# Other staging space for the second half of the latent tiles, and other release points for turned keys, queries and values

## The chip, the cores and the metric

One Trainium2 chip; the program runs on 8 cores, each with its own share of the work and none waiting for another. The time of a run is that of the slowest core, in device microseconds. A profile of one execution is at hand, and three timed runs.

## The reference

One layer of a hybrid diffusion transformer, cut to what matters:

```python
sh1, sc1, g1, sh2, sc2, g2 = adaln(c, w_ada, b_ada)      # silu(c) @ w_ada + b_ada, in six parts
h = rms_norm(x, norm1_w) * (1 + sc1) + sh1
q, k, v, u, g = split(h @ w_in)                          # 1024, 1024, 1024, 1024, 1024 columns
q, k = rope(rms_norm64(q)), rope(rms_norm64(k))          # the context's: no rope; its k and v are outputs
# 8 heads, each with two softmax maps of 64 dimensions; latents read their own and 256 cached keys
att = sublayer_rms((softmax(q1 @ k1.T / 8) - lam * softmax(q2 @ k2.T / 8)) @ v)
sgu = gelu(u) * (w_s @ layer_norm(gelu(g)) + b_s)        # in chunks of 128 positions
x = x + g1 * (concat(att, sgu) @ w_o)
h = rms_norm(x, norm2_w) * (1 + sc2) + sh2
x = x + g2 * (square(relu(h @ w_ff1)) @ w_ff2)
```

There are 16 context sequences of 256 tokens and 4 latent sequences of 2048, model width 2048. Two cores share a latent sequence: each computes the outputs of its own 1024 latent tokens and of two context sequences.

## The kernel before, in words

**Tiles.** A core has 12 own tiles of 128 tokens: 0 to 3 context, 4 to 11 its own latents. For attention it also needs keys and values of the *other half* of its latent sequence, tiles 12 to 19. These are loaded (`x_load`), normed (`norm_x`: a square on ScalarE with its sum, a reciprocal root, a scale on ScalarE, VectorE or GpSimd), transposed on TensorE and modulated (`late_group`, groups of two: 12, 14, 16, 18) into `hO`, and projected to keys and values only. `group_ev[t]` tells that group t stands in `hO`, `xnev[t]` that tile t is normed.

**Stages.** First modulation (`ada0`: 8 units of 4 pieces of weights, from a ring of 6 buffers of 4 KB per partition at address b0) beside the first projection (`proj0`), which runs over four quarters of the contraction and keeps partial sums of pair 0's keys and queries (`KU`), and of pair 0's and 1's values (`VU`), in SBUF; `drained[...]` tells that such a sum has been read for the last time. Then the four groups of the other half with pair 0's k and v, and pair 1's values by `late_v1` wherever TensorE has time (priority 15; `proj0` has 14, the smaller number goes first). Then for the pairs of heads 0 to 3 `attention(p)` beside `proj(p+1)`; then the gates, the output projection and the MLP. The weights for `proj(1)` go where those of `proj0` were: each block of 1 MB is loaded when group 18's matmuls with the old one are through.

**Turns.** A projected and normed key or query tile lies in one of 8 buffers (`kr`) and is transposed by a DMA of SyncE, a *turn* (`S.turn`), into `KT[s]` or `QT[s]`; s is the pair's number modulo 2. `VV[s]` holds values. Before a turn (or a write of values) for pair p >= 2 the chain waits for `att_end[p-2]`, that is all of attention p-2 with its last `finalize`. `sc_end[p]` is the end of its scores, `av_done[p]` that of its products with values.

**Space.** Slot 0 at b0 holds KT0 (11 KB), QT0 (6 KB), VV0 (11 KB); slot 1 behind it, KT1, QT1, VV1, then z1 and p1. `xt` are the loads' buffers (8 KB each), `xn` those of normed tiles (4 KB). For tiles 12 to 19 the buffers come one after the other from the pools in `xpool`: `xta` (xt0, under `hO[3]`), `xtb` (xt1, under `hO[2]`, once four partial sums of values are drained), `xtp` (xt4 and xt5 at p1, under the probabilities, once keys' and queries' sums are drained). The loads leave from one thread in the order of the tiles; GpSimd issues them.

**Order.** Nothing is ordered by hand: `Sched` simulates threads with costs in ns while the program is built. A thread posts instructions to engines; each engine takes the one of least priority number that is ready in the simulation, and that order is fixed in the program. On the chip each engine runs its list in order, and semaphores are derived from the memory that instructions read and write. A turn is costed at 300 + 1.7 ns per element of a row, a transfer at 315 B/ns, and a turned tile of pair 0 counts as there 8 us after its turn (`TURN_SLACK`).

Lines that matter: L586 issues loads, L591 stores, L597 turns; L455 is every matmul, L465 every transpose of TensorE; L488 ScalarE, L510 and L517 VectorE, L543 GpSimd's scale.

Of the kernel before, what the change touches and what calls it, by code (L numbers as in the profile page):

```python
# [9 lines left out]
F32 = mybir.dt.float32  # L10
BF16 = mybir.dt.bfloat16
# [4 lines left out]
D = 2048  # L16
# [4 lines left out]
K = 1024  # L21
SB = 16512
# [600 lines left out]
def build_program():  # L623
# [34 lines left out]
    S = Sched(nc)  # L658
# [4 lines left out]
    def bank(j):  # L663
        return PS[:, j * 512:(j + 1) * 512]
# [44 lines left out]
    b0 = SB + 118 * K  # L709
    KT, QT, VV = [], [], []  # L710
    for i in range(2):
        b = b0 + i * SLOT
# [3 lines left out]
    slot1 = b0 + SLOT  # L716
    z1 = b0 + 2 * SLOT
# [16 lines left out]
    NPART = 6  # L734
    ada = [S.sbuf("ada%d" % i, [128, 4, 512], BF16, b0 + i * 4 * K) for i in range(NPART)]
    adas = Pool(S, range(NPART))
    xt = [S.sbuf("xt%d" % i, [128, D], F32, b) for i, b in enumerate((SB + 86 * K, SB + 78 * K, slot1 + 17408, z1 + 4 * K, p1, p1 + 8 * K))]
    xts = Pool(S, range(4))
    xta, xtb, xtp = Pool(S), Pool(S), Pool(S)
    xpool = [xts] * 12 + [xta, xtb, xta, xtb, xtb, xta, xta, xtp]  # L740
    xn = [S.sbuf("xn%d" % i, [128, D], BF16, slot1 + i * 4 * K) for i in (2, 3, 0, 1)]
    xns, xno = Pool(S, range(4)), Pool(S)
    mod0 = S.sbuf("mod0", [128, 512], F32, z1)
    cT_t = S.sbuf("cT_t", [128, 16, 2], F32, z1 + 2048)
# [17 lines left out]
    def evs(n):  # L762
        return [Ev() for _ in range(n)]
# [11 lines left out]
    ada_ev, xev, xnev, raw_ev = [evs(4) for _ in range(8)], evs(20), evs(20), evs(12)  # L775
    mod_ev, h_ev = evs(4), [evs(3) for _ in range(4)]
    sc_ev, ident_ev, const_ev, tab_ev, lam_ev = Ev(), Ev(), Ev(), Ev(), Ev()
    own_x, ho_free, slot1_ev, wr2_ev, ada_out = Ev(), evs(4), Ev(), Ev(), Ev()
    group_ev = {t: Ev() for t in range(12, 20, 2)}
    W0 = {(k, b): Ev() for k in ("k0", "v0", "q0", "v1") for b in range(4)}  # L780
# [63 lines left out]

    def staging():
        xta.give(0)
        yield [drained[k] for k in VU[:4]]
        xtb.give(1)
        yield [drained[k] for k in KU[:4]]
        xtp.give(4)  # L850
        yield [drained[k] for k in KU[4:8]]
        xtp.give(5)
        yield [drained[k] for k in KU[8:]]
        xno.give(2)
        xno.give(3)
        yield xnev[12:20] + [group_ev[18]]
        slot1_ev.fire()
# [41 lines left out]
    def ada0():  # L899
        yield [sc_ev, const_ev]  # L900
        for u in range(8):
            j = yield banks
            for i in range(4):
                yield ada_ev[u][i]
                op = ada_mm(ada[adabuf[u, i]], bank(j), 512, range(4 * i, 4 * i + 4), 4 * i)
                op.then(lambda u=u, i=i: adas.give(adabuf[u, i]))
            yield op
            yield S.copy(mod0, bank(j))
            yield from ada_cols(mod0, bank(j), 512, 1 if u % 2 == 0 else 0, (u // 2) * 4, 0)
            banks.give(j)  # L910
            if u % 2 == 1:
                mod_ev[u // 2].fire()
# [73 lines left out]
    def chain_qk(b, kind, t0, p, op):  # L986
# [71 lines left out]
                yield S.spawn(rope(zn, kind, t0 - 4, rb if early else None), 23 if p else RP + (1 if kind == 'q' else 0))  # L1058
            stats.give(st)
        dst = QT[s] if kind == "q" else KT[s]  # L1060
        yield att_end[p - 2 if p >= 2 else 4]
        if p == 1:
            yield slot1_ev
        yield S.turn(dst[:, t0:t0 + 2].rearrange("p t h n -> p (t h) n"), zn, "kr%d" % kj)
        krs.give(kj)
        if p == 0:
# [42 lines left out]

    def chain_v(b, t0, p, op):  # L1110
        s = p % 2
        yield [op, att_end[p - 2 if p >= 2 else 4]]
        dst = VV[s][:, t0:t0 + 2, :, 0:128]
        v4 = lambda a: a.rearrange("p (t h d) -> p t h d", t=2, h=2)
        sv_rows = sv[t0 * 128:(t0 + 2) * 128, p * 256:(p + 1) * 256].rearrange("(t p) n -> p t n", p=128) if t0 < 4 else None
        if t0 < 4:
            vf = yield outs[p]
            yield S.copy(vf, bank(b))
            banks.give(b)
            yield S.copy(dst, v4(vf))  # L1120
        else:
            yield S.copy(dst, v4(bank(b)))
            banks.give(b)
        VVev[p][t0 // 2].fire()
        if t0 < 4:
            S.store(sv_rows, vf.rearrange("p (t n) -> p t n", t=2), "sk").then(lambda: S.at(STORE_SLACK if p else 0.0, lambda: outs[p].give(vf)))

    def cached(p):
        s = p % 2
        yield att_end[p - 2 if p >= 2 else 4]  # L1130
        if p == 1:
            yield own_x
        ops = [S.memset(VV[s][:, :, :, 128:130], 1.0)]
        for t in range(2):
            ops.append(S.load(VV[s][:, 20 + t, :, 0:128], cv[t * 128:(t + 1) * 128, p * 256:(p + 1) * 256].rearrange("p (h d) -> p h d", d=128),
                              "cv%d" % t, cast=True))
        kj = yield krs
        ops.append(S.load(kr[kj].rearrange("p (t n) -> p t n", t=2), ck[:, p * 256:(p + 1) * 256].rearrange("(t p) n -> p t n", p=128),
                          "ck", cast=True))
        yield ops  # L1140
        VVev[p][10].fire()
        yield S.turn(KT[s][:, 20:22].rearrange("p t h n -> p (t h) n"), kr[kj], "kr%d" % kj)
        krs.give(kj)
        KTev[p][10].fire()
# [79 lines left out]
        op.then(v_done.fire)  # L1224

    def half_free(h):
        yield [drained[k] for k in VU[4 * h + 4:4 * h + 8]] if h < 2 else xnev[12:17] if h == 2 else xnev[12:19]
        ho_free[h].fire()

    ORD = "kqv"  # L1230
# [107 lines left out]
    def attention(p):  # L1338
        s = p % 2
        yield [sc_end[p - 1], QTev[p][0], tab_ev]  # L1340
        if p == 0:
            yield [proj_end[0]] + xnev
            for i in range(3):
                Ps.give(i)
            yield (banks, range(6))
# [10 lines left out]
        def av():  # L1356
            yield av_done[p - 1]
            n = 0
            while n < len(items):
                if not todo:  # L1360
                    more[0] = Ev()
                    yield more[0]
                    continue
                its, pj, es = todo.popleft()
                yield [VVev[p][it[2] // 2] for it in its] + es
                ops = []
                for j, (hh, q0, kt, first, last) in enumerate(its):
                    if first:
                        if ops:
                            S.mm(ops)  # L1370
                            ops = []
                        yield Otok
                    for m in range(2):
                        for i in range(2):
                            ops.append((O[m][:, i * 130:i * 130 + 129], Pt[pj][:, m, j * 256 + i * 128:j * 256 + (i + 1) * 128],
                                        VV[s][:, kt, hh, 0:129], first and i == 0, last))
                    if last:
                        op = S.mm(ops)
                        ops = []
                        fin.append(S.spawn(finalize(2 * p + hh, q0, op), 8))  # L1380
                if ops:
                    op = S.mm(ops)
                op.then(lambda pj=pj: Ps.give(pj))
                n += len(its)

        av_end = S.spawn(av(), 10.5)
        for i0 in range(0, len(items), 4):
# [67 lines left out]
    def gates():  # L1455
# [11 lines left out]
        for n, (nb, t0) in enumerate(GORD):  # L1467
            yield wev[4, nb]
            w = wslot[4, nb]
            if t0 < 4:  # L1470
                yield att_end[2]
            j = yield banks
            for i in range(2):
                for k0 in range(0, 16, 4):
# [438 lines left out]
```

How the kernel before makes its waits and increments, by code:

```python
    def add(self, eng, fn, reads=(), writes=(), key=None, dr=(), dw=()):  # L204
# [63 lines left out]
            for s, v in nd.snap.items():  # L268
                if known.get(s, 0) < v:
                    known[s] = v
            known[nd.sem] = nd.val
        E = self.eng[eng]
        wl = list(waits.items())
        attach = None
        if eng != "pe" and wl:
            attach = wl.pop()
        for s, v in wl:
            E.wait_ge(self.sems[s], v)
        ins = fn(E)
        if attach:
            ins._wait_ge(self.sems[attach[0]], attach[1])
        nd = Node()
        nd.eng = eng
        nd.dma = dma
        if dma:
            name = "d_" + key
            if name not in self.sems:
                self.sems[name] = self.nc.alloc_semaphore(name)
                self.dcnt[name] = 0
            self.dcnt[name] += 1
            ins.then_inc(self.sems[name], 16)
            nd.sem, nd.val = name, 16 * self.dcnt[name]
        else:
            self.cnt[eng] += 1
            ins.then_inc(self.esem[eng], 1)
            nd.sem, nd.val = "c_" + eng, self.cnt[eng]
        nd.snap = dict(known)
        i = len(self.nodes)
# [301 lines left out]
    def wait_all_stores(self, keys):  # L600
        for k in keys:
            nd = self.nodes[self.dlast[k]]
            if self.known["sp"].get(nd.sem, 0) < nd.val:
                self.nc.sync.wait_ge(self.sems[nd.sem], nd.val)
```

## Time and profile before

| what | value |
|---|---|
| three timed runs | 2464.01, 2472.96, 2458.88 us; median 2464.01 |
| the profiled execution | 2466.38 us |
| its span on the slowest core, core 4 | 2465.3 us |
| spans of all cores | 2444.4 to 2465.3 us |
| TensorE matmul busy | 2366.6 us (96%) |
| VectorE, ScalarE, GpSimd busy | 1120.7 (45%), 729.1 (30%), 232.5 us (9%) |
| DMA | 251.58 MB, mean 102 GB/s |

Shares are means over the whole span: TensorE is far less busy in the first 300 us than after. L12 is line 12 of the kernel. "PE" is TensorE's matmul, "PEld" its weight load, "DVE" VectorE, "ACT" ScalarE, "POOL" GpSimd, "SP" SyncE, "SPq" a DMA issue on SyncE. Releasers of waits are inferred from semaphores.

### The profile page before, as it was taken

The numbers are of one execution on the slowest core, as the hardware profiler recorded it, in microseconds if no ns is written. First come the engines' busy times: TensorE is split into PE (matmuls) and PEld (weight loads), VectorE is DVE, ScalarE is ACT, GpSimd is POOL, SyncE is SP. The second block draws the span as 40 slices with busy tenths as digits, with TensorE's granted clock in tenths as the row PEclk, the third lists the DMA queues.
The fourth block names the chain that finished last, engine by engine and source line by source line (L and its number), as shares of the span: only waits on it lengthen the run. The fifth ranks groups of instructions, "written<-read, shape, count | busy, mean of one in ns | idle before, by whom it ended". The sixth has DMA issues, their size and how long they took to land.

```text
span 2465.3 us, 38569 instructions; the slowest of 8 cores (2444.4 to 2465.3 us)
## 1 busy us (share of the span) xinstructions
PE 2366.6 (96%) x16224; PEld 1357.6 (55%) x16224; DVE 1120.7 (45%) x2216; ACT 729.1 (30%) x1196; POOL 232.5 (9%) x394
## 2 busy tenths in 40 slices
PE   3689799999999999999999999999999999999999
PEld 2568687878888854444444444444444444444444
DVE  2567776744742154554101332322524616528347
ACT  2515576766756561222231001001010010010110
POOL 1213311111111030000110000000000000000000
PEclk9799899999999999999999999999999999999999
DMA  9995978967754285976563333333433434434346
GB/s 217 191 170 139 120 97 90 128 95 111 117 85 85 45 125 134 241 210 129 93 108 52 52 52 52 52 52 52 90 65 60 89 55 71 80 51 84 63 96 187
DMA packets 168729, 251.58 MB, mean 102 GB/s; under 512 B 101104, under 2 KB 106864, under 8 KB 154480
## 3 DMA queue, kind: packets, MB, share of 16 engines
q0 software_dynamic: 54816, 169.14, 42.3%
q1 hardware_dynamic: 113744, 79.97, 14.0%
q8 instruction: 132, 2.16, 0.4%
q14 instruction: 37, 0.30, 0.0%
HBM read 348.28 MB, written 32.67 MB: 155 GB/s over the span
## 4 chain that ended last, share of the span: by engine, by line
PE 91%; DMA 5%; DVE 2%; ACT 1%; issue 0%; POOL 0%; SPq 0%
PE ps L455 91%; DMA ada<-wa 2%; DMA QT<-kr 1%; DMA sk<-t 1%; DMA xt<-xp 1%; PE ps L465 1%; DMA wr<-wa 1%; DVE hT L517 0%; DVE xn L517 0%; DMA tab<-rsin 0%; ACT xn L488 0%; DMA sv<-t 0%; DVE t L510 0%; ACT hO L488 0%; POOL xn L543 0%
## 5 line engine op out<-in xcount | busy, mean ns | idle before, releaser
L455 PE MATMUL ps<-wf,aT 128*128 128x512 bf16 x3072 | 665.0, 379 | 0.0
L455 PE MATMUL ps<-hT,wf 128*128 128x512 bf16 x3072 | 665.0, 379 | 0.0
L455 PEld LDWEIGHTS ps<-wf,aT 128*128 128x128 bf16 x3072 | 300.3, 98 | 362.3 <-issue 0.8
L455 PEld LDWEIGHTS ps<-hT,wf 128*128 128x128 bf16 x3072 | 300.2, 98 | 362.4 <-issue 0.8
L488 ACT ACTIVATE tm<-ps 128x512 f32<-128x512 f32 x192 | 114.4, 597 | 1030.0 <-PE ps L455 1030.0
L510 DVE TENSOR_TENSOR aT<-tm 128x512 bf16<-128x512 f32 x192 | 132.7, 692 | 549.3 <-ACT tm L488 546.5
L455 PE MATMUL ps<-wr,hT 128*128 128x256 bf16 x2880 | 356.7, 280 | 19.6 <-DVE hT L517 15.8
L488 ACT ACTIVATE P<-ps 128x1024 bf16<-128x1024 f32 x304 | 296.5, 1020 | 148.6 <-PE ps L455 148.5
L455 PEld LDWEIGHTS ps<-wr,hT 128*128 128x128 bf16 x2880 | 280.8, 100 | 70.5 <-issue 33.9
L510 DVE TENSOR_TENSOR acc<-acc,ps 128x512 f32<-128x512 f32 x216 | 148.4, 687 | 154.2 <-PE ps L455 153.8
L455 PE MATMUL ps<-VV,P 128*128 128x129 bf16 x2432 | 166.0, 221 | 6.2 <-issue 3.3
L510 DVE TENSOR_TENSOR tm<-ps,g_t 128x512 f32<-128x512 f32 x168 | 115.9, 690 | 95.1 <-PE ps L455 94.9
L455 PEld LDWEIGHTS ps<-VV,P 128*128 128x128 bf16 x2432 | 141.8, 98 | 30.3 <-issue 29.7
L586 POOL DMA_DIRECT2D wf<-wf x64 | 33.9, 530 | 1185.1 <-PE ps L455 1150.7
L455 PE MATMUL ps<-wr,hO 128*128 128x256 bf16 x1024 | 121.3, 273 | 1.3 <-ACT hO L488 0.8
L455 PEld LDWEIGHTS ps<-wr,hO 128*128 128x128 bf16 x1024 | 97.2, 98 | 16.3 <-issue 5.8
L455 PE MATMUL ps<-QT,KT 64*128 64x256 bf16 x1216 | 93.2, 272 | 2.2 <-ACT P L488 1.8
L455 PE MATMUL ps<-hT,wu 128*128 128x512 bf16 x384 | 85.8, 379 | 0.0
L455 PE MATMUL ps<-wo,sguT 128*128 128x512 bf16 x384 | 84.8, 379 | 0.0
L510 DVE TENSOR_TENSOR acc<-acc,tm 128x512 f32<-128x512 f32 x120 | 82.9, 691 | 3.6
L586 POOL DMA_DIRECT2D wr<-wa x96 | 51.3, 551 | 297.2 <-PE ps L455 296.9
L465 PE MATMUL ps<-identb,xn 128*128 128x128 bf16 x320 | 30.3, 270 | 43.3 <-DVE xn L517 29.8
(177 smaller groups left out, 1610.9 us busy)
## 6 DMA issues: line engine op xcount, KB each, us to landing
wf<-wf POOLq DMA_DIRECT2D x64, 1024.0 KB, 9.9
wr<-wa POOLq DMA_DIRECT2D x96, 256.0 KB, 7.5
ada<-wa POOLq DMA_DIRECT2D x32, 512.0 KB, 22.0
xt<-xs POOLq DMA_DIRECT2D x16, 1024.0 KB, 8.8
x1d<-xw SPq DMA_DIRECT2D x12, 1024.0 KB, 5.7
x1b<-x1d SPq DMA_DIRECT2D x48, 256.0 KB, 3.0
wr<-wqkv POOLq DMA_DIRECT2D x44, 256.0 KB, 11.2
wo<-wo POOLq DMA_DIRECT2D x32, 256.0 KB, 9.9
```

What stands on the lines that cost most here:

```text
L455: ins = e.matmul(o, lhsT=l, rhs=r, start=st, stop=sp, skip_group_check=True)
L465: ins = e.transpose(o, i, ident)
L488: "act", lambda e: e.activation(out=out, in_=in_, func=func, bias=bias, scale=scale, **kw),
L510: return self.post(eng, cost, lambda: self.add(eng, lambda e: e.tensor_tensor(out=out, in0=a, in1=b, op=op), reads=[a, b], writes=[out]), ...
L586: eng, lambda e: e.dma_start(out=out, in_=src), writes=[out], key=key, dr=dr), 0, nbytes=nb, prio=prio)
```

## The change

* The fifth load buffer `xt4` moves from p1 to b0, where the first two ring buffers of the modulation are (later KT0); `xt5` goes. A pool `xtc` hands it out when the last modulation matmul is through (`ada_done`). Tiles 12 to 19 come from xta, xtc, xtb, xtc, xta, xtb, xtc, xta.
* Two more buffers for normed tiles, xn4 and xn5, at b0 + 8 KB and b0 + 12 KB (later the end of KT0, and QT0), also from `ada_done` on.
* So the turns of pair 0 wait: early keys for `xnev[18]`; queries, late keys and the cached key for `group_ev[18]`. `hO[2]` and `hO[3]` become free one normed tile later. `attention(0)` waits for all of `KU` to be drained.
* For pairs 2 and 3 turns wait for `sc_end[p-2]`, writes of values for `av_done[p-2]`, the gates' first tiles for `av_done[2]`; `av_done` now follows the end of the last product.

```diff
--- before.py
+++ after.py
@@ -734,11 +734,12 @@
     NPART = 6
     ada = [S.sbuf("ada%d" % i, [128, 4, 512], BF16, b0 + i * 4 * K) for i in range(NPART)]
     adas = Pool(S, range(NPART))
-    xt = [S.sbuf("xt%d" % i, [128, D], F32, b) for i, b in enumerate((SB + 86 * K, SB + 78 * K, slot1 + 17408, z1 + 4 * K, p1, p1 + 8 * K))]
+    xt = [S.sbuf("xt%d" % i, [128, D], F32, b) for i, b in enumerate((SB + 86 * K, SB + 78 * K, slot1 + 17408, z1 + 4 * K, b0))]
     xts = Pool(S, range(4))
-    xta, xtb, xtp = Pool(S), Pool(S), Pool(S)
-    xpool = [xts] * 12 + [xta, xtb, xta, xtb, xtb, xta, xta, xtp]
+    xta, xtb, xtc = Pool(S), Pool(S), Pool(S)
+    xpool = [xts] * 12 + [xta, xtc, xtb, xtc, xta, xtb, xtc, xta]
     xn = [S.sbuf("xn%d" % i, [128, D], BF16, slot1 + i * 4 * K) for i in (2, 3, 0, 1)]
+    xn += [S.sbuf("xn%d" % i, [128, D], BF16, b0 + (4 * i - 8) * K) for i in (4, 5)]
     xns, xno = Pool(S, range(4)), Pool(S)
     mod0 = S.sbuf("mod0", [128, 512], F32, z1)
     cT_t = S.sbuf("cT_t", [128, 16, 2], F32, z1 + 2048)
@@ -775,6 +776,7 @@
     ada_ev, xev, xnev, raw_ev = [evs(4) for _ in range(8)], evs(20), evs(20), evs(12)
     mod_ev, h_ev = evs(4), [evs(3) for _ in range(4)]
     sc_ev, ident_ev, const_ev, tab_ev, lam_ev = Ev(), Ev(), Ev(), Ev(), Ev()
+    ada_done = Ev()
     own_x, ho_free, slot1_ev, wr2_ev, ada_out = Ev(), evs(4), Ev(), Ev(), Ev()
     group_ev = {t: Ev() for t in range(12, 20, 2)}
     W0 = {(k, b): Ev() for k in ("k0", "v0", "q0", "v1") for b in range(4)}
@@ -844,12 +846,12 @@
 
     def staging():
         xta.give(0)
+        yield ada_done
+        xtc.give(4)
+        xno.give(4)
+        xno.give(5)
         yield [drained[k] for k in VU[:4]]
         xtb.give(1)
-        yield [drained[k] for k in KU[:4]]
-        xtp.give(4)
-        yield [drained[k] for k in KU[4:8]]
-        xtp.give(5)
         yield [drained[k] for k in KU[8:]]
         xno.give(2)
         xno.give(3)
@@ -905,6 +907,8 @@
                 op = ada_mm(ada[adabuf[u, i]], bank(j), 512, range(4 * i, 4 * i + 4), 4 * i)
                 op.then(lambda u=u, i=i: adas.give(adabuf[u, i]))
             yield op
+            if u == 7:
+                ada_done.fire()
             yield S.copy(mod0, bank(j))
             yield from ada_cols(mod0, bank(j), 512, 1 if u % 2 == 0 else 0, (u // 2) * 4, 0)
             banks.give(j)
@@ -1058,9 +1062,11 @@
                 yield S.spawn(rope(zn, kind, t0 - 4, rb if early else None), 23 if p else RP + (1 if kind == 'q' else 0))
             stats.give(st)
         dst = QT[s] if kind == "q" else KT[s]
-        yield att_end[p - 2 if p >= 2 else 4]
+        yield sc_end[p - 2 if p >= 2 else 4]
         if p == 1:
             yield slot1_ev
+        if p == 0:
+            yield group_ev[18] if kind == "q" or t0 >= 12 else xnev[18]
         yield S.turn(dst[:, t0:t0 + 2].rearrange("p t h n -> p (t h) n"), zn, "kr%d" % kj)
         krs.give(kj)
         if p == 0:
@@ -1109,7 +1115,7 @@
 
     def chain_v(b, t0, p, op):
         s = p % 2
-        yield [op, att_end[p - 2 if p >= 2 else 4]]
+        yield [op, av_done[p - 2 if p >= 2 else 4]]
         dst = VV[s][:, t0:t0 + 2, :, 0:128]
         v4 = lambda a: a.rearrange("p (t h d) -> p t h d", t=2, h=2)
         sv_rows = sv[t0 * 128:(t0 + 2) * 128, p * 256:(p + 1) * 256].rearrange("(t p) n -> p t n", p=128) if t0 < 4 else None
@@ -1127,7 +1133,7 @@
 
     def cached(p):
         s = p % 2
-        yield att_end[p - 2 if p >= 2 else 4]
+        yield av_done[p - 2 if p >= 2 else 4]
         if p == 1:
             yield own_x
         ops = [S.memset(VV[s][:, :, :, 128:130], 1.0)]
@@ -1139,6 +1145,8 @@
                           "ck", cast=True))
         yield ops
         VVev[p][10].fire()
+        if p == 0:
+            yield group_ev[18]
         yield S.turn(KT[s][:, 20:22].rearrange("p t h n -> p (t h) n"), kr[kj], "kr%d" % kj)
         krs.give(kj)
         KTev[p][10].fire()
@@ -1224,7 +1232,7 @@
         op.then(v_done.fire)
 
     def half_free(h):
-        yield [drained[k] for k in VU[4 * h + 4:4 * h + 8]] if h < 2 else xnev[12:17] if h == 2 else xnev[12:19]
+        yield [drained[k] for k in VU[4 * h + 4:4 * h + 8]] if h < 2 else xnev[12:18] if h == 2 else xnev[12:20]
         ho_free[h].fire()
 
     ORD = "kqv"
@@ -1339,7 +1347,7 @@
         s = p % 2
         yield [sc_end[p - 1], QTev[p][0], tab_ev]
         if p == 0:
-            yield [proj_end[0]] + xnev
+            yield [proj_end[0]] + xnev + [drained[k] for k in KU]
             for i in range(3):
                 Ps.give(i)
             yield (banks, range(6))
@@ -1382,6 +1390,7 @@
                     op = S.mm(ops)
                 op.then(lambda pj=pj: Ps.give(pj))
                 n += len(its)
+            yield op
 
         av_end = S.spawn(av(), 10.5)
         for i0 in range(0, len(items), 4):
@@ -1468,7 +1477,7 @@
             yield wev[4, nb]
             w = wslot[4, nb]
             if t0 < 4:
-                yield att_end[2]
+                yield av_done[2]
             j = yield banks
             for i in range(2):
                 for k0 in range(0, 16, 4):
```

## Rows read from the trace of the kernel before

**Rows 1.** Spans and granted clock of the cores, the slowest.
```profile
core 4: 2465.3 us, clock 0.986
```

**Rows 2.** Stretch, length, busy PE, PEld, DVE, ACT, POOL; clock, DMA share, GB/s.
```profile
200.00:230.00 30.00, 26.79 (x252) 23.92 (x250) 21.89 (x46) 19.30 (x40) 14.00 (x11) 0.89 0.49 151
230.00:260.00 30.00, 22.32 (x217) 19.53 (x216) 21.51 (x34) 21.03 (x47) 10.22 (x8) 0.91 0.61 115
260.00:300.00 40.00, 31.38 (x270) 24.81 (x269) 31.47 (x72) 20.66 (x46) 18.16 (x22) 0.88 1.07 112
...
400.00:600.00 200.00, 195.30 (x2444) 157.44 (x2444) 110.17 (x342) 134.53 (x204) 36.20 (x66) 0.99 0.75 104
600.00:800.00 200.00, 199.99 (x2408) 164.16 (x2405) 102.60 (x311) 128.72 (x199) 26.29 (x48) 1.00 0.61 98
```

**Rows 3.** TensorE's waits, 200 to 274 us: total, times, longest.
```profile
PE ps L465 <- ACT st L498: 6.2, 1, 6.2
PE ps L465 <- POOL xn L543: 3.2, 1, 3.2
PE ps L465 <- DVE xn L517: 1.1, 1, 1.1
```

**Rows 4.** TensorE in time: start, us, instructions, [idle before, releaser].
```profile
207.63 2.72 PE L465 MATMUL ps<-identb,xn 128*128 128x128 bf16 x24 [3.21 <-POOL xn L543]
...
224.90 11.95 PE L455 MATMUL ps<-wr,hO 128*128 128x256 bf16 x108
237.98 1.95 PE L465 MATMUL ps<-identb,xn 128*128 128x128 bf16 x32 [1.13 <-DVE xn L517]
...
258.13 3.41 PE L465 MATMUL ps<-identb,xn 128*128 128x128 bf16 x32 [6.24 <-ACT st L498]
...
279.36 7.76 PE L455 MATMUL ps<-wr,hT 128*128 128x256 bf16 x44 [2.35 <-DMA wr<-wqkv]
287.51 0.61 PE L455 MATMUL ps<-QT,KT 64*128 64x256 bf16 x8 [0.38 <-DMA QT<-kr]
```

**Rows 5.** TensorE's waits, 274 to 306 us.
```profile
PE ps L455 <- DMA wr<-wqkv: 3.4, 2, 2.4
PE ps L455 <- DVE ot L549: 2.7, 1, 2.7
```

**Rows 6.** GpSimd in time: its loads of x and one norm.
```profile
164.92 0.58 POOL L586 DMA_DIRECT2D xt<-xs  x1
191.47 0.53 POOL L586 DMA_DIRECT2D xt<-xs  x1 [25.97 <-DVE VV L510]
...
202.05 5.44 POOL L543 TENSOR_SCALAR xn<-xt,st 128x2048 bf16<-128x2048 f32 x1 [5.78 <-ACT st L498]
...
221.74 1.13 POOL L586 DMA_DIRECT2D xt<-xs  x2 [3.45 <-DVE xn L517]
```

**Rows 7.** Loads of x: landings of 60 to 320, then of 236 to 256 us.
```profile
DMA to landing us min/median/max: 5.2/7.5/22.8
...
L586 POOL DMA_DIRECT2D xt<-xs x2: 528/566/603, 238.1 to 239.3; - x2
...
DMA to landing us min/median/max: 9.8/11.7/13.5
```

**Rows 8.** VectorE in time: the last value sum of group 12's space.
```profile
204.13 0.69 DVE L510 TENSOR_TENSOR t<-ac_0v,ps 128x512 f32<-128x512 f32 x1 [1.74 <-DMA sv<-t]
```

**Rows 9.** Core 6, TensorE's waits, 180 to 420 us.
```profile
PE ps L455 <- DMA wr<-wqkv: 7.2, 2, 5.1
```

**Rows 10.** Turns: one issued at 266.7 us, then those of 269 to 286 us.
```profile
DMA to landing us min/median/max: 2.3/2.3/2.3
...
L597 SPq DMA_TRANSPOSE QT<-kr x4: 1190/1326/1502, 269.6 to 284.2; - x4
...
  DVE kr L510: 5.2, 1
...
DMA to landing us min/median/max: 13.2/15.5/17.8
```

## The prediction

> **What bounds the kernel now.** I read the spans and clocks of the cores first: core 4 is the slowest at 2465.3 us [rows 1]. The profiled execution took 2466.4 us, so 1.1 us lie outside the span; the median of the runs shown, 2464.0, is 2.4 us lower. The sum below is made for core 4 against 2466.4, and the 2.4 us are taken off at the end.
>
> Next came the busy time by stretches [rows 2]. From 600 us on TensorE is busy in 200.0 of 200 us, so whatever is saved ahead of that arrives whole at the end, and the later stretches read the same; nothing can be saved there by freeing a buffer. Between 200 and 300 us it is busy 26.8 + 22.3 + 31.4 = 80.5 of 100 us: 19.5 us stand open, at a granted clock of 0.88 to 0.91, that is for the most part at the upper of its two levels (2.4 GHz) and for some microseconds at the lower (1.2 GHz). This is where the tiles of the other half of the latents (x12 to x19) are normed, transposed and multiplied.
>
> Then the waits of TensorE in that stretch. Ahead of the transposes of groups 12, 14 and 18 it waits 3.2 + 1.1 + 6.2 = 10.5 us for normed tiles [rows 3]. The timeline puts them at 207.6, 238.0 and 258.1 us [rows 4]. After the last group it waits 3.4 us for the first weights of pair 1, 2.7 us for the attention's output accumulator [rows 5], and 0.4 us for a turned query ahead of the first score at 287.5 [rows 4].
>
> Why are the normed tiles late? GpSimd's timeline of loads [rows 6]: x12 is issued at 164.9 us. x13 waits 26.0 us, until 191.5, because its space (xt1) lies under four partial sums of values. x16 and x17 leave at 221.7, x18 and x19 at 238.1 and 239.3 [rows 7], each when a buffer has been normed (x19 when partial sums of keys have been drained). A load lands 5.2 us after its issue at best, 7.5 in the median [rows 7]. So two staging buffers, used by turns, set the pace; the DMA is not full (busy share 0.49 and 0.61 by the page's measure in those stretches [rows 2]).
>
> **The change, part by part.**
>
> 1. *A third staging buffer and two more places for normed tiles, in the ring of the first modulation.* xt4 moves to b0 and is free at ada_done, the end of the last modulation matmul. The last piece for that matmul is issued ahead of x12, on the same queue, and x12 lands at 164.9 + 22.8 = 187.7 [rows 6, 7]; so ada_done falls between 165 and 188, and I take 180. Then x13 leaves near 180 instead of 191.5, x14 near 191.5 as x13 did. With three buffers in turn and some 5.5 us for each load, x19 lands at about 187.7 + 7 x 5.5 = 226 us, against 239.3 + 13.5 = 252.8 [rows 6, 7]. The norms take about 4 us more each: x19 is ready at 230 or a little later, while TensorE, at 2 us of transposes and three projections of some 3.5 us (32 x 0.11, from 108 matmuls in 11.95 us [rows 4]) per group, comes to group 18 at 205 + 3 x 12.5 = 242 us. The wait of 6.2 and that of 1.1 us go: 7.4 us. Group 12 was held by a norm that GpSimd took for 5.44 us, until 207.5 [rows 6]; next late is the space of its output, which waits for the partial sum of a value that VectorE drains at 204.13 + 0.69 = 204.8 [rows 8]. I count 207.6 - 204.9 = 2.7 us. Bounds for these three waits: 3 us saved (the late norms of ScalarE and VectorE remain) to 10.5.
>
> 2. *The clock behind these waits.* After the two long ones the transposes run slower: at 207.6 us 24 took 2.72 us, 32 took 3.41 us at 258.1, where 32 took 1.95 us after a wait of 1.1 [rows 4]. That is 1.3 + 1.5 = 2.8 us, saved if the waits fall under some 1 us; bounds 0 and 5 (the projections right behind are slow as well).
>
> 3. *Weights of pair 1.* Their space comes free at group 18's last key projection, and only v18 and one late projection of pair 1's values cover the load. If tiles arrive ahead of TensorE, those late projections (priority 15, after 14) are left for the end and cover it. At stake: 3.4 us [rows 5] and the slow matmuls behind, 44 in 7.76 us instead of 44 x 0.11 = 4.9 [rows 4], 2.9 us; 6.3 in all. The other end: core 6 waits 7.2 us here today, 3.8 more than core 4 [rows 9]. I take 4 us saved, nearer to the gain, since the order by priority speaks for the cover.
>
> 4. *Turns wait longer.* Turned keys of pair 0 wait for xnev[18]; queries, the four late keys and the cached key for group_ev[18]. By part 1 xnev[18] comes at about 222 to 228, some 20 us ahead of the last group, so the six early keys are out of the way by then. Of the six queries four are turned from 269.6 on today [rows 10]. Now six queries, k12, k14, k16, k18 and the cached key, eleven turns, leave in one run after the last group. What is queued behind: SyncE's other stores (none urgent), and the chains that hold the 8 kr buffers; VectorE already stood 5.2 us for one [rows 10]. A turn alone lands in 2.3 us; the four issued between 269.6 and 284.2, beside three blocks of weights, took 13.2 to 17.8 [rows 10]. Cost between 0 (TensorE has pair 1's projections as filler, and everything is 12 us earlier) and 15 (see the second rival). I take 3, near the waits of 0.4 + 2.7 us of today.
> The Trainium skill says in "DMA: Bandwidth & Descriptors", Queues, rings and completion order, that an SDMA engine takes turns between queue rows packet by packet, so a turn with small packets gets a small part beside large loads. The trace agrees (2.3 against 13.2 to 17.8 us). By that rule the turns that start before the weights are quick and those behind them slow; with the 3 us counted for them the sum below is 13.9 us, and with turns that are never slowed 16.9.
>
> 5. *Attention of pair 0 also waits for all early keys and queries to be drained; its first probabilities no longer share space with x18 and x19.* Today the first score waits 0.4 us for a turned query [rows 4], so the drains behind these turns are earlier still. With kr buffers held longer the drains of the last queries follow the first key turns, at about 240 to 250, ahead of the end of projection 0 (about 260). Nothing; if it were late, projections of pair 1 cover it. Bounds 0 and 3.
>
> 6. *sc_end and av_done for att_end (pairs 2 and 3, first gate tiles), and the step that waits for the last value product.* These open buffers one finalize earlier, at 500 us and later, where TensorE has no open time [rows 2]. Between 400 and 600 it is open for 4.7 us [rows 2], and a buffer of attention could have been behind 2 of them at most. Nothing; bounds 2 saved, 1 lost, since instructions change their order.
>
> Sum: 7.4 + 2.7 + 2.8 + 4 - 3 = 13.9 us. 2466.4 - 13.9 = 2452.5, less 2.4: **2450 us**, 0.57% faster. The whole of the 19.5 open us and the slow clock would be some 25.
>
> **The rivals.**
>
> *The pace is not set by space.* Norms wait in the queues of ScalarE and VectorE (the 6.2 us are put down to ScalarE's statistics [rows 3]), and GpSimd may again be given a norm of 5.4 us. For it: VectorE is busy 21.9 and 21.5 of 30 us there [rows 2]. Against it: those statistics came 2 us after a tile that landed at 252.8. Then about half of parts 1 and 2 comes, 5 to 6 us, and part 3 stays away: 2459.
>
> *The waits move behind the last group, turned slower.* Mechanism: eleven turns leave at group_ev[18] at once, collide with the weights that are issued 4 us later, hold all 8 kr buffers, and each projection of pair 1 then keeps its bank. Price: the four turns issued from 269.6 to 284.2 are 4.9 us apart [rows 10]; eleven at that pace take 54 us. TensorE has at most 8 banks x 3.5 = 28 us of work without a free kr. So 26 us open at most and some 3 for the slow matmuls behind, 13 us won ahead: 2464 + 29 - 13 = 2480. It costs something from 28 / 11 = 2.5 us per turn on and makes the kernel slower from (28 + 13) / 11 = 3.7 on, if no kr comes free in between. Against it: the four turns under that load cost TensorE 0.4 us today, and each turn that lands does release a kr. A third of this, 8 to 10 us lost with part 3's gain gone, gives 2459 and no measurable change.
>
> The slowest core may be another one afterwards; that shifts the result by 2 or 3 us and is in the range.
>
> **How the numbers follow.** Forecast (2443 to 2457): 0.58. Pace not by space, 2459: 0.16. Turns pile up, mild, 2459: 0.16. Piled up fully, 2480: 0.10. The bound of "no change" is 0.5%, 12.3 us: 2451.7 to 2476.3. Of the forecast's 0.58 some 0.48 lies below 2451.7, as its open ends (part 2's slow projections, all of part 3) lie on that side; with a little of the others 0.50 is faster, 0.40 the same, 0.10 slower. The range 2438 to 2468 takes in both cases at 2459 and leaves out the fully piled one and a gain of over 26 us.
>
> **What would show it.** Right: GpSimd issues x13 near 180 us and x19 before 215; TensorE's waits ahead of transposes sum to under 2 us; two or more late value projections stand behind group 18's keys; busy TensorE over 200 to 300 us rises from 80 to 90 or more; first score near 270. Wrong in part 1: x19 lands in time and the transposes still wait for ScalarE or GpSimd. Wrong in part 4: new waits of over 5 us for kr, QT or KT between 255 and 300 us, or a granted clock under 0.8 there. Wrong in part 6: fewer open microseconds of TensorE from 400 us on than today, or open time after 600.

## The result

The changed kernel is slower: the ratio of its times to those of the kernel before is 1.0063, with a 95% interval from 1.0041 to 1.0085, that is about 15 us more. The medians of 20 runs each are 2486.66 and 2473.07 us; the ratio leaves out runs that were disturbed (one die longer, at a lower granted clock), but of the 15 runs of the changed kernel that it keeps eight stand at 2483.6 to 2487.9 us with cores at a clock of 0.966 to 0.977, while none that it keeps of the kernel before is above 2473.2, so the 15 us are probably too many. I ran the changed kernel once more beside the experiments: 1.0044 (1.0028 to 1.0061), 11 us more, which is the better mark. The forecast was 2450 us, 0.57% less, and the time lies outside the range.

The profiled execution took 2466.88 us, 2465.8 of it in the span of core 4, the slowest core again. These are the spans and granted clocks by core:

```profile
core 4: 2465.8 us, clock 0.987
die 0 (median of its cores): 2460.7 us, clock 0.986
die 1 (median of its cores): 2462.1 us, clock 0.988
```

Core 4 had 2465.3 us before [rows 1], so the slowest core alone shows nothing. The median cores do: 2460.7 and 2462.1 us against 2451.9 and 2452.5, some 9 us more. One must look at all cores where 0.5% is at stake.

The busy time by stretches of core 4 comes next (us, busy time and count of PE, PEld, DVE, ACT, POOL, granted clock, DMA share, GB/s):

```profile
200.00:230.00 30.00, 23.37 (x245) 21.30 (x243) 25.56 (x44) 19.48 (x40) 25.92 (x13) 0.90 0.58 189
230.00:260.00 30.00, 29.35 (x285) 25.96 (x284) 27.43 (x50) 18.65 (x47) 18.42 (x13) 0.99 0.29 63
260.00:300.00 40.00, 26.77 (x249) 23.34 (x250) 25.97 (x42) 9.02 (x26) 12.21 (x16) 0.90 1.05 112
400.00:600.00 200.00, 191.13 (x2403) 155.10 (x2400) 106.50 (x335) 138.02 (x208) 36.02 (x65) 0.98 0.74 107
600.00:800.00 200.00, 199.94 (x2443) 163.50 (x2441) 101.18 (x316) 131.70 (x197) 25.03 (x47) 1.00 0.57 90
```

Against [rows 2] the second stretch is now nearly full (29.4 us busy instead of 22.3), the third has lost that (26.8 instead of 31.4), and 400 to 600 us stands open for 8.9 us instead of 4.7. From 600 us on both are all but full, so whatever is lost before arrives at the end, as the prediction said. Worked out from such rows, the mean open time of TensorE over the eight cores, in us, is this (e2 and the others are experiments below):

| stretch | before | after | e2 | e3 | e9 | e10 | e11 |
|---|---|---|---|---|---|---|---|
| 200:250 | 6.3 | 7.6 | 6.9 | 8.3 | 6.5 | 7.4 | 7.3 |
| 250:300 | 11.6 | 9.8 | 7.2 | 13.3 | 10.0 | 4.2 | 7.4 |
| 300:420 | 1.2 | 2.4 | 3.0 | 1.8 | 0.5 | 1.1 | 0.3 |
| 420:470 | 0.0 | 7.5 | 8.3 | 0.2 | 0.9 | 4.6 | 0.0 |
| 470:600 | 1.1 | 0.1 | 1.3 | 0.2 | 0.5 | 0.1 | 1.2 |
| 600:2440 | 2.1 | 3.2 | 2.7 | 4.8 | 7.6 | 3.8 | 4.5 |

From 200 to 600 us that is 20.2 us before and 27.4 after; the mean span grew by 7.1 us. The rise of the mean span is in this table, and on balance it stands in 420:470, a stretch to which the prediction gave nothing; the rises and falls of the other stretches cancel. The timeline of TensorE on core 4 (start, duration, tile, shapes, in brackets the idle time before and its releaser) shows both places:

```profile
226.96 2.72 PE L465 MATMUL ps<-identb,xn 128*128 128x128 bf16 x24 [6.63 <-POOL xn L543]
267.17 19.81 PE L455 MATMUL ps<-wr,hT 128*128 128x256 bf16 x180 [1.35 <-DMA wr<-wqkv]
286.81 1.47 PE L455 MATMUL ps<-wr,hO 128*128 128x256 bf16 x12
299.75 1.05 PE L455 MATMUL ps<-wr,scT 128*32 128x256 bf16 x16 [11.47 <-DVE t L558]
303.13 11.85 PE L455 MATMUL ps<-wr,hO 128*128 128x256 bf16 x96
314.91 0.61 PE L455 MATMUL ps<-QT,KT 64*128 64x256 bf16 x8
...
445.18 0.61 PE L455 MATMUL ps<-QT,KT 64*128 64x256 bf16 x8 [1.10 <-ACT P L488]
447.96 0.61 PE L455 MATMUL ps<-VV,P 128*128 128x129 bf16 x8 [1.61 <-DVE ot L549]
453.81 1.04 PE L455 MATMUL ps<-wr,scT 128*32 128x256 bf16 x16 [4.69 <-DVE st L517]
```

The first score stands at 314.9 us and not at 287.5 [rows 4]; over the cores it moved from 269 to 288 us to 306 to 316. Ahead of it TensorE stands idle for 11.5 us behind VectorE. Near 445 us attention(0) runs with no projection of pair 1 left to fill its waits for probabilities and finalizes.

VectorE's timeline tells why it was late at 288 us: it waits for turned queries five times, 13.2 us in all, since the buffers `kr` are held. These are the three longest:

```profile
278.10 0.69 DVE L510 TENSOR_TENSOR kr<-ps,st 128x512 bf16<-128x512 f32 x1 [3.21 <-DMA QT<-kr]
283.88 0.69 DVE L558 CAST kr<-ps 128x512 bf16<-128x512 f32 x1 [3.21 <-DMA QT<-kr]
289.83 0.69 DVE L558 CAST kr<-ps 128x512 bf16<-128x512 f32 x1 [2.80 <-DMA QT<-kr]
```

The query turns themselves, issued between 256.9 and 279.4 us (times to issue in ns; last line the landing), take as long as the slowest of before [rows 10], and now all six do:

```profile
L597 SPq DMA_TRANSPOSE QT<-kr x6: 1189/1270/3562, 256.9 to 279.4; - x6
...
DMA to landing us min/median/max: 11.9/16.9/19.0
```

They lie beside three blocks of weights, whose issues GpSimd's timeline has at 255.66, 259.71 and 266.22. The timelines of SyncE and GpSimd for core 4 of the kernel before have the same turns and the first of these blocks here:

```profile
258.96 26.43 SPq L597 DMA_TRANSPOSE QT<-kr  x6
267.79 2.19 POOL L586 DMA_DIRECT2D wr<-wqkv  x4
```

So the query turns did not gather into one moment: the first and the last leave 22.5 us apart after, 25.2 before, even if the first three now leave within 3 us. On all eight cores group 18 stands in `hO` some 5.5 us ahead of the first query turn, and that turn leaves as soon as VectorE has written its `kr`. For core 4 VectorE's timeline has these two, and the turn follows at 256.9 us:

```profile
250.94 0.41 DVE L517 TENSOR_SCALAR hO<-ps,A,S 128x256 bf16<-128x256 bf16 x1 [0.63 <-ACT hO L488]
256.19 0.68 DVE L510 TENSOR_TENSOR kr<-ac_0q,qkw_t 128x512 bf16<-128x512 f32 x1
```

The new wait for `group_ev[18]` thus did not hold the first query on the chip at its turn. What moved most is the weights: on core 4 the first block leaves 12 us earlier, ahead of all six query turns and not behind the second, and the projections of pair 1, which need `kr`, start at 264 us and not at 274. In the mean of the cores the first block leaves 7 us earlier (255.1 us, not 262.0) and the first query turn 3 us later (256.3, not 253.3), since its `kr` is written later. The turns that were held are those of keys: on core 4 they leave from 236 us on and not from 221, seven of them by 253. Whether their `kr` buffers make the queries late, no run shows.

GpSimd's timeline also holds the loads and norms of the other half:

```profile
178.40 0.54 POOL L586 DMA_DIRECT2D xt<-xs  x1 [13.12 <-PE ps L455]
188.95 0.53 POOL L586 DMA_DIRECT2D xt<-xs  x1 [10.02 <-DVE VV L510]
197.14 1.05 POOL L586 DMA_DIRECT2D xt<-xs  x2 [7.65 <-DVE xn L517]
199.22 5.44 POOL L543 TENSOR_SCALAR xn<-xt,st 128x2048 bf16<-128x2048 f32 x1 [1.03 <-ACT st L498]
204.97 0.58 POOL L586 DMA_DIRECT2D xt<-xs  x1 [0.30 <-POOL xn L543]
210.60 6.64 POOL L543 TENSOR_SCALAR xn<-xt,st 128x2048 bf16<-128x2048 f32 x1 [0.96 <-ACT st L498]
217.20 1.14 POOL L586 DMA_DIRECT2D xt<-xs  x2
220.85 5.97 POOL L543 TENSOR_SCALAR xn<-xt,st 128x2048 bf16<-128x2048 f32 x1
230.86 5.44 POOL L543 TENSOR_SCALAR xn<-xt,st 128x2048 bf16<-128x2048 f32 x1 [1.56 <-ACT st L498]
255.66 2.21 POOL L586 DMA_DIRECT2D wr<-wqkv  x4
259.71 2.19 POOL L586 DMA_DIRECT2D wr<-wqkv  x4
266.22 2.17 POOL L586 DMA_DIRECT2D wr<-wa  x4
```

The loads did come earlier, as forecast (x13 at 178.4 instead of 191.5, the last two at 217.2 instead of 238.1 and 239.3 [rows 6, 7]), but GpSimd was given four norms where it had one at 202 [rows 6].

### The profile page after: what moved, and what is told of

The parts are those of the page before. It is cut to its first block, busy times and chain, and to the rows that moved or that the text cites. A ratio compares the mean times of both kernels' runs of the same rounds, so it can differ in the third digit from the quotient of the medians.

```text
span 2465.8 us, 38556 instructions; the slowest of 8 cores (2453.0 to 2465.8 us)
## 1 busy us (share of the span) xinstructions
PE 2362.0 (96%) x16224; PEld 1355.7 (55%) x16224; DVE 1129.1 (46%) x2215; ACT 725.9 (29%) x1193; POOL 251.3 (10%) x398
## 4 chain that ended last, share of the span: by engine, by line
PE 91%; DMA 4%; DVE 3%; ACT 1%; issue 0%; POOL 0%; SPq 0%; ACTq 0%
PE ps L455 91%; DMA QT<-kr 1%; DMA ada<-wa 1%; DMA xt<-xp 1%; DMA KT<-kr 1%; PE ps L465 1%; DVE xn L517 0%; DVE hT L517 0%; DVE t L510 0%; DVE kr L510 0%; DMA tab<-rsin 0%; ACT hO L488 0%; DVE st L562 0%; POOL xn L543 0%; DVE hO L517 0%
## 5 line engine op out<-in xcount | busy, mean ns | idle before, releaser
L455 PEld LDWEIGHTS ps<-wr,hO 128*128 128x128 bf16 x1024 | 99.3, 99 | 14.7 <-issue 2.9
L455 PEld LDWEIGHTS ps<-QT,KT 64*128 64x128 bf16 x1216 | 47.4, 94 | 37.1 <-issue 32.6
```

The source lines that it names most:

```text
L455: ins = e.matmul(o, lhsT=l, rhs=r, start=st, stop=sp, skip_group_check=True)
```

## The experiments

The ratio is to the kernel before, timed beside each run, with its 95% interval. What the expectations call theory A is this: the gate of part 5 (all of `KU` drained) makes attention(0) ask for its six banks later, when the projections of pair 1 have already taken them. So the first score comes late, more of pair 1's projection is done ahead of it, and that filler is missing at 420 to 470 us. Its rivals are that GpSimd's norms cost the time (theory B), that held `kr` buffers do (theory C, part 4), and that the new release points do (part 6).

**e1: the change again.**

> The changed kernel as it is, timed again beside the others of this job; nothing is edited. Every theory expects the ratio of before: slower by 0.4 to 0.9% (10 to 20 us), the first score of attention(0) after 305 us, a wait of TensorE of 7 to 12 us around 290 us, and 5 to 9 us of open time between 435 and 455 us.

1.0044 (1.0028 to 1.0061). Open time by stretch as in the table, 7.7 us in 420:470. This is the mark for what follows.

**e2: the gate of part 5 alone, in the kernel before.**

```diff
-            yield [proj_end[0]] + xnev
+            yield [proj_end[0]] + xnev + [drained[k] for k in KU]
```

> The kernel before with one line of the change: attention(0) also waits for all early keys and queries to be drained before it asks for its six banks. Theory A (late claim: by then proj(1) has taken the banks, each held by a tile that waits for a kr buffer, so attention starts late and proj(1)'s matmuls, which should fill its gaps, are used up early) expects 8 to 12 us slower than before, a first score at 300 us or later instead of 287.5, and open time of TensorE of 5 us or more near the end of attention(0). Theory B (GpSimd's norms of 5.4 us and more) and theory C (turns that pile up behind the last group) expect no change within 3 us, since norms and turns stay as they were.

1.0020 (1.0008 to 1.0032), 4.9 us. The first score moved to 298 to 313 us, and 8.3 us stood open in 420:470. On the slowest core, core 0, the timeline reads:

```profile
311.94 0.61 PE L455 MATMUL ps<-QT,KT 64*128 64x256 bf16 x8
...
441.45 0.61 PE L455 MATMUL ps<-QT,KT 64*128 64x256 bf16 x8 [1.10 <-ACT P L488]
446.97 1.02 PE L455 MATMUL ps<-VV,P 128*128 128x129 bf16 x8 [1.61 <-DVE ot L549]
459.24 0.58 PE L455 MATMUL ps<-sel_t,modl 128*128 128x2 f32 x4 [1.94 <-DVE modl L558]
```

The mechanism of theory A is there from one added wait, but its price by the timed ratio is half of what I expected: less is open near 270 us (7.2 us in 250:300, not 11.6). What share of the loss it is remains unclear. By the ratios it is 4.9 of 11 us; by the open time from 200 to 600 us (26.7 us, against 20.2 before and 27.4 after) it is nearly all of it.

**e3: the change, with the banks asked for first.**

```diff
-        yield [sc_end[p - 1], QTev[p][0], tab_ev]
         if p == 0:
-            yield [proj_end[0]] + xnev + [drained[k] for k in KU]
+            yield [proj_end[0]] + xnev
+            yield (banks, range(6))
+            yield [drained[k] for k in KU]
             ...
-            yield (banks, range(6))
+        yield [sc_end[p - 1], QTev[p][0], tab_ev]
```

> The changed kernel, but attention(0) asks for its six banks at the end of projection 0, ahead of its waits for the first turned query, the drained sums and the tables. Theory A expects the first score at 290 us or earlier, no open time between 435 and 455 us, and 10 to 18 us less than the changed kernel: level with before or up to 8 us faster. Theory C expects the wait of some 11 us at 290 us to stay, or to stand ahead of the first scores instead, and a gain over the changed kernel of under 5 us. Theory B expects the wait ahead of group 14's transposes (6.6 us) to stay, whatever else goes.

1.0007 (0.9991 to 1.0023). The open time of 420:470 is gone (0.2 us) and the first score is back at 276 to 291 us. But now TensorE waits for `kr` in front of the attention, and 250:300 is open for 13.3 us, more than in either kernel. On core 0, the slowest:

```profile
290.69 1.04 PE L455 MATMUL ps<-QT,KT 64*128 64x256 bf16 x8 [7.28 <-DVE kr L510]
296.40 3.79 PE L455 MATMUL ps<-wr,hT 128*128 128x256 bf16 x20 [4.67 <-DVE kr L558]
```

This is 9 us less than e1, where I expected 10 to 18. So the change no longer loses, yet its staging space still brings nothing: TensorE now waits 9.7 us for `kr` in the mean of the cores.

**e4: the new release points of part 6 alone, in the kernel before** (`sc_end` and `av_done` for `att_end`, and the step that waits for the last product). **e12: the change without them.**

```diff
-        yield att_end[p - 2 if p >= 2 else 4]
+        yield sc_end[p - 2 if p >= 2 else 4]
         ...
-        yield [op, att_end[p - 2 if p >= 2 else 4]]
+        yield [op, av_done[p - 2 if p >= 2 else 4]]
         ...
```

> The kernel before with only the new release points: turns of pairs 2 and 3 after sc_end, writes of values after av_done, av_done at the end of the last product. The prediction's part 6 and theories A to C expect no change within 3 us and no open time of TensorE from 400 us on beyond that of before (4.7 us to 600 us). If the release points are the cause of the new open time at 435 to 455 us, it shows here and costs 5 us or more.

> The changed kernel with the old release points (turns and writes of pairs 2 and 3 wait for all of attention two pairs back, av_done as before). The prediction's part 6 says no difference from the changed kernel within 2 us. A rival: since attention(0) ends late in the changed kernel, the last finalize now holds turns of pair 2 and the old points cost 3 to 6 us more, with open time beyond 420 us.

e4: 1.0003 (0.9991 to 1.0015). e12: 1.0031 (1.0019 to 1.0042), not to be told from e1. Part 6 makes no difference beyond the intervals, and that rival is out.

**e5: the change with no norm of tiles 12 to 19 on GpSimd. e6: the same with the banks of e3.**

```diff
-            yield S.scale(xn[j], xt[b], st[:, 1:2])
+            yield S.affine(xn[j], xt[b], st[:, 1:2], None)
```

> The changed kernel, but the scale of a normed tile 12 to 19 goes to ScalarE or VectorE only. Theory B (GpSimd takes 5.4 to 6.6 us for a norm that the schedule costs at 2.0 us, and the transposes of group 14 wait for it) expects the wait of 6.3 to 7 us to go, and 5 to 8 us less than the changed kernel, so 3 to 6 us over before. Theory A (late claim of the banks) expects the first score to stay after 300 us and the open 7 to 8 us between 420 and 470 us to stay, so at most a part of the loss goes; if the late claim were the bound of all, the time would stay within 3 us of the changed kernel.

> The changed kernel with both edits: banks claimed at the end of projection 0, norms on ScalarE or VectorE only. Theories A and B together expect the sum of both gains: 4 to 8 us less than with the claim alone (which stood 1.7 us over before), so 3 to 7 us under before. Theory C (turns that pile up) expects its price, the waits of TensorE for kr buffers between 280 and 305 us (12 us on the slowest core with the claim alone), to stay, so no more than 5 us under before.

e5: 1.0012 (1.0000 to 1.0023). That is 8 us less than e1, as theory B expected, so GpSimd's norms did cost in the changed kernel. The wait ahead of the transposes went (open time in 200:250 from 7.6 to 3.4 us), and a part of it came back behind the first projections of pair 1, at the place where the changed kernel waits 11.5 us (250:300 was open for 14.3 us). The timeline of TensorE on core 2 reads:

```profile
299.76 0.62 PE L455 MATMUL ps<-wr,scT 128*32 128x256 bf16 x8 [18.24 <-ACT st L498]
```

e6: 1.0020 (1.0009 to 1.0031). I had added the gains of e3 and e5; they do not add. The stretch 250:300 was open for 19.5 us, and on the slowest core, core 7, its waits were:

```profile
PE ps L455 <- DVE kr L510: 14.6, 1, 14.6
PE ps L465 <- DVE ac_0k L510: 8.7, 1, 8.7
```

The first stands on every core, 13.8 us in the mean; the second, ahead of transposes, on this core alone. The earlier TensorE arrives, the longer it stands in front of the same held buffers. That is what a wait does whose end is set elsewhere; I take it to be the turns, and e8 bears on that.

**e7: turns held as in the change, in the kernel before**, with the banks asked for first.

```diff
         dst = QT[s] if kind == "q" else KT[s]
+        if p == 0:
+            yield group_ev[18] if kind == "q" or t0 >= 12 else xnev[18]
         ...
```

> The kernel before, its staging space unchanged, but turns of pair 0 are held as in the change (early keys until the normed tile 18, queries, late keys and the cached key until group 18 stands in its space), and the banks are claimed at the end of projection 0. Theory C expects waits for kr or turned tiles of 5 to 12 us between 270 and 305 us beyond those of before and 4 to 8 us more than before. Theory A, with the claim early, expects no loss beyond 3 us.

1.0025 (1.0014 to 1.0035), 6 us. Near the end of projection 0 TensorE waits for turned queries 4.3 us in the mean (3.1 us on core 0), against 1.0 before, and 1.0 us for `kr`. Yet from 200 to 600 us it stands open for no more than before (19.0 us against 20.2); what is added is a wait for a turned query near 690 us, 4.5 us in the mean, where neither kernel has any. e9 has the same wait without holding a turn, and no run claims the banks early in the kernel before, so this run does not show that holding the turns costs by itself.

**e8: the change with the edits of e3 and e5, and the weights behind the query turns.** The block for pair 1's queries and the first weights that the second modulation puts into the ring (`wr<-wa`) wait until all six query tiles of pair 0 are turned:

```diff
+    turned0 = {(k, t): Ev() for k in "kq" for t in range(0, 20, 2)}
...
             krs.give(kj)
             if p == 0:
+                turned0[kind, t0].fire()
                 yield TURN_SLACK
...
+    qturned = [turned0["q", t] for t in range(0, 12, 2)]
         for p, k in blocks:
             j = yield w_free
+            if (p, k) == (1, "q"):
+                yield qturned
...
-        yield v_done
+        yield [v_done] + qturned
```

> As the kernel with both edits (early claim, no norms on GpSimd), and the second block of pair 1's weights and the first block of the second modulation are loaded only when the six queries of pair 0 have been turned. Theory C with its cause in the DMA (turns of 13 to 18 us beside loads, 2.3 us alone) expects query turns that land within 6 us, the waits for kr buffers between 280 and 305 us cut to under 4 us, and 4 to 8 us less than without this edit: 8 to 14 us under before. If the turns are slow by themselves, nothing changes within 2 us.

0.9964 (0.9948 to 0.9979), faster than both kernels and, at 9 us under before, in the expected range. The six query turns of core 2 now land in half the time or less, if not within the 6 us that I expected (14.3 us in the median on that core in the changed kernel):

```profile
L597 SPq DMA_TRANSPOSE QT<-kr x6: 1189/1643/3836, 254.6 to 272.4; - x6
...
DMA to landing us min/median/max: 2.8/6.9/10.2
```

**e9: late weights in the kernel before. e10: late weights alone in the change.** Both have the last edit only.

> The kernel before with one edit: the second block of pair 1's weights and the first of the second modulation are loaded only when the six queries of pair 0 are turned. Theory C (turns are slow because loads run beside them) expects 2 to 6 us less than before, out of the waits for the output accumulator, for queries and for pair 1's first weights. If this equals the 9 us of the kernel with all three edits, the staging space itself is worth nothing; the theory that earlier tiles do help expects 3 us or more between the two.

> The changed kernel with that edit alone: banks still claimed late, norms still on GpSimd. Theory C expects the wait of 8 to 11 us for kr buffers near 290 us to go, 5 to 8 us less than the changed kernel, so 3 to 6 us over before. Theory A expects the first score to stay at 295 us or later and 5 to 8 us open between 420 and 470 us, since the banks are claimed as late as in the change.

e9: 1.0008 (0.9997 to 1.0019). I expected a gain and there is none. But the edit does two things here. Until 600 us TensorE stands open for 18.4 us and not 20.2, and its waits for turned queries there (1.0 us in the mean) are gone; later each core has a new wait for a turned query, 5.2 us in the mean, on core 2 this:

```profile
692.88 0.99 PE L455 MATMUL ps<-QT,KT 64*128 64x256 bf16 x8 [4.99 <-DMA QT<-kr]
```

So in the kernel before the collision costs under 2 us of open time by 600 us, and the ratio alone does not give its price. Why the late wait arises is open.

e10: 0.9969 (0.9957 to 0.9980). I expected 5 to 8 us less than the change and a kernel still slower than before. It is 0.75% under e1, 18 us, and 15 us under e12, which was timed side by side with it. This one edit turns the sign of the whole change. Its turns, its weights and its first score on core 7:

```profile
L597 SPq DMA_TRANSPOSE QT<-kr x6: 1175/1491/3630, 259.6 to 277.1; - x6
...
DMA to landing us min/median/max: 5.3/9.2/14.7
```

```profile
273.29 2.21 POOL L586 DMA_DIRECT2D wr<-wqkv  x4
275.46 2.15 POOL L586 DMA_DIRECT2D wr<-wa  x4
```

```profile
302.56 0.61 PE L455 MATMUL ps<-QT,KT 64*128 64x256 bf16 x8 [4.30 <-ACT kr L488]
```

The two blocks that left at 259.7 and 266.2 us in the change (core 4) leave at 273.3 and 275.5, and the turns' median falls from 16.9 to 9.2 us; on cores 0, 2, 4 and 7 it is 14.3 to 16.9 us in the change and 8.6 to 9.2 here. The wait of 11.5 us on core 4 becomes one of 4.7 there and 4.3 on core 7, in the mean of the cores 6.9 becomes 4.1. The gate is still in, and as theory A says the first score is still late (294 to 304 us) and 420:470 is open for 4.6 us.

**e11: the change with the edits of e3 and e10.**

> The changed kernel with the early claim and the late weights, norms still on GpSimd. Theories A and C expect neither the open time at 420 to 470 us nor waits for kr; theory B expects the wait of 6 to 7 us for GpSimd's norm ahead of group 14 to stay, so 2 to 6 us more than with all three edits (which stood 9 us under before), that is 3 to 7 us under before.

0.9961 (0.9948 to 0.9975), 9.6 us less than before, where I expected 3 to 7. Table above: nothing is left in 420:470, the first score is at 273 to 280 us. Waits for `kr` are left against my expectation, 6.4 us in the mean. With GpSimd's norms still in it, it equals e8 without them within the intervals.

## Why the prediction was wrong

**Part 4 is the step that failed.** It said "I take 3, near the waits of 0.4 + 2.7 us of today", with bounds of 0 and 15. Moving two of the three blocks of weights out of the way of the turns gives back 15 us by the ratios that were timed side by side (e10 against e12; 18 against e1). Of these the profiles show 11 as open time of TensorE (32.6 us open from 200 us to 2440 in e12, 21.2 in e10, in the mean of the cores), and the mean spans are 14.9 us apart. The wait that results is that of my second rival, to which I gave 0.10 for its full form: the turns are slow beside the weights and hold the `kr` buffers, VectorE stands in line for them (13.2 us in five waits), the banks stay taken, and TensorE waits 11.5 us. The way into it is another than I wrote. The turns did not leave together at the last group; each query's left when its `kr` was written, over 22 us. The last group was done earlier, which is part 1's gain, so the weights left earlier (7 us in the mean, 12 on core 4) while the first query turn did not (3 us later in the mean), and the loads now lie beside all six query turns instead of four. I argued against the rival that "the four turns under that load cost TensorE 0.4 us today". e9 agrees that the cost was small in the kernel before (under 2 us of open time until 600 us), and that is beside the point: I took a cost that is nearly zero today as the measure of what it would be. That enough `kr` were left for pair 1's first tiles before is my reading; no run counts them.

What e10 leaves untested is a rival of another kind: the edit also changes the order that is fixed while the program is built. On core 4 TensorE does 80 matmuls `ps<-wr,hO` ahead of its wait near 300 us in e10 and 12 in the change. The landing times of the turns speak for the collision, but no run moves the weights and keeps the order. So the cause is shown as far as the place of the two loads goes; that it works through the turns is read from the traces.

The rule of the Trainium skill that I weighed there ("DMA: Bandwidth & Descriptors", Queues, rings and completion order: engines take turns between queue rows packet by packet) agrees with these traces: query turns land in 11.9 to 19.0 us beside the loads, in 5.3 to 14.7 and 2.8 to 10.2 with two of the three blocks behind them. My sentence on it said that turns starting before the weights are quick; but all six query turns of core 4 start behind the first block, at 256.9 to 279.4 us against 255.7.

**Part 5 was sized at nothing and cost 4.9 us (e2).** It put the last drain of a query's sum at 240 to 250 us, ahead of the end of projection 0. The row that I took for this, the turned query of the first score, does not bear on it: VectorE reads the last such sum only 4 us ahead of that score in the kernel before, and at 278.7 us after, when projection 0 has been through for 15 us.

```profile
283.44 0.68 DVE L510 TENSOR_TENSOR kr<-ac_0q,st 128x512 bf16<-128x512 f32 x1
278.71 0.68 DVE L510 TENSOR_TENSOR kr<-ac_0q,st 128x512 bf16<-128x512 f32 x1
```

And I did not look for what else happens meanwhile. `proj(1)` asks for banks at the same moment, and in an order fixed while the program is built one late request reorders the 150 us behind it. "Projections of pair 1 cover it" was the error: they cover it by being used up, and are missing at 420:470. Which of parts 4 and 5 weighs more in the change can't be told: claiming the banks first gives back 9 of its 11 us (e3), norms without GpSimd 8 (e5), the weights 15 to 18 (e10). The three do not add.

**Part 1 was right on the loads and wrong on what they bring as things stood.** The tiles came 13 to 21 us earlier. The mean wait of TensorE in 200:265 fell only from 9.8 to 8.1 us, not by the 10.1 of my terms on core 4, since GpSimd norms four tiles at 5.4 to 6.6 us each: my first rival, given 0.16. What the space is worth by itself is not shown. With late weights the changed kernel is 0.3 to 0.4% under the kernel before (e10, e11) and e9, without the space, is not; but 5.2 of the 9.6 us between e9 and e10 are e9's wait near 690 us, and until 600 us the two stand open for 18.4 and 17.4 us. **Part 2** came by half: 24 transposes take 2.72 us at 227.0 as they did at 207.6, but the slow ones of group 18 (3.41 us at 258.1 [rows 4]) are gone. **Part 3** was not gained: the mean wait for pair 1's weights went from 3.0 to 3.1 us. **Part 6** at nothing was right (e4, e12).

The sign that I had named for part 4 came, if under another name: there was to be a new wait of over 5 us for `kr`, QT or KT between 255 and 300 us, and the wait of 11.5 us is put down to VectorE's copy `t`, which stands behind five waits for `kr`. For more open time from 400 us on I had named no sign. The claim held that all of a loss before 600 us arrives at the end.

What stays open: how the loss splits between the late claim, the norms and the collision, since each edit alone takes away most of it; where the wait near 690 us in e7 and e9 comes from; what fixed order and collision each do in e10; and part 3's own share. No experiment took away the norms of GpSimd and the weights' collision without also moving the banks.

## What to carry to other kernels

When a change lets a large load leave earlier, look up which small transfers will now lie beside it, count the buffers they hold, and ask when the last of these runs out; a latency that costs little today says little of the same transfers once their users come earlier. A large load that can wait should be queued behind the small transfers that others wait for: here one such condition turned the changed kernel from slower than before to faster, though in the kernel before it brought nothing. An added wait ahead of a request for banks costs the place in the queue as well as its own length, and filler work used up early shows as open time much later. Gains of edits that touch one chain of waits must be measured together: here they did not add.

## What was unexpected of the hardware

A turn of 128x512 bf16 that lands in 2.3 us alone [rows 10] took 16.9 us in the median, up to 19.0, while 1 MB blocks of weights ran. GpSimd's norm of a 128x2048 tile took 5.44 us twice and 6.64 and 5.97 us in the other two cases. A change of 0.4 to 0.6% in the timed ratio left the slowest core's profiled span the same within 0.5 us, and the medians of both dies 9 us apart.
